# One row product by halves, first units by tiles, norm spread one unit later: three reorderings in a 256-token two-block network on Trainium2

## The reference

```python
def _rmsnorm(x, g):
    y = xf * lax.rsqrt(jnp.mean(xf * xf, axis=-1, keepdims=True) + RMS_EPS)
    return (y * g)

def _swiglu(h, w_in, w_out):
    gate, up = jnp.split(h @ w_in, 2, axis=-1)
    return (jax.nn.silu(gate) * up) @ w_out

for i in range(DEPTH):            # nsa mixer, then wkv mixer
    ...
    x = x + jnp.concatenate([mix, cross], axis=-1) @ w_o[i]
    x = x + _swiglu(_rmsnorm(x, norm2[i]), w_ffn_in[i], w_ffn_out[i])
x = _rmsnorm(x, final_norm)
...                               # second_block: mixer, then
h = rmsnorm(x, ffn_pre_g[l])
x = x + rmsnorm(swiglu(h, w_gate[l], w_up[l], w_down[l]), ffn_post_g[l])
```

## Time and profile before

| what | value |
|---|---|
| median of 3 runs | 1194.93 us (1193.71 to 1199.79) |
| the profiled execution | 1196.21 us, span 1194.4 us |
| granted TensorE clock, mean | 0.988 of full |
| PE busy | 1158.1 us (97%) |
| DVE busy | 758.2 us (63%) |
| ACT busy | 603.2 us (51%) |
| chain that ended last | PE 87%, DVE 6%, ACT 3%, DMA 2%, issue 1% |

### The profile page before, as it was taken

One profiled execution on the slowest core, in us unless ns is written; L12 is line 12 of the kernel. 1 busy time (PEld: TensorE's weight loads), 2 busy tenths in 40 slices (PEclk: granted clock), 3 DMA queues, 4 the chain that ended last, 5 costly groups with the idle time before them and its releaser, 6 DMA issues.

```text
span 1194.4 us, 23500 instructions
## 1 busy us (share of the span) xinstructions
PE 1158.1 (97%) x9992; PEld 1079.9 (90%) x9992; DVE 758.2 (63%) x1292; ACT 603.2 (51%) x1029; POOL 32.0 (3%) x46
## 2 busy tenths in 40 slices
PE   6999999999999999999999999999999999999997
PEld 6999888999988988898789998889999998999986
DVE  5575656676736668766667675475754676767644
ACT  4665555444434673434354544364358755444533
POOL 0000000000000010340000000000000000000000
PEclk9999999999999998999899999999999999999999
DMA  9843124876554533001488765546654444777651
GB/s 280 247 128 103 71 72 137 225 198 190 199 188 146 178 106 106 3 3 39 112 217 219 202 188 204 182 119 203 183 183 127 140 144 127 191 201 188 202 186 71
DMA packets 218916, 185.38 MB, mean 155 GB/s; under 512 B 11266, under 2 KB 204048, under 8 KB 218684
## 3 DMA queue, kind: packets, MB, share of 16 engines
q1 hardware_dynamic: 217226, 181.50, 50.6%
q0 software_dynamic: 384, 1.05, 0.4%
q10 hardware_dynamic: 1202, 1.34, 0.3%
HBM read 181.77 MB, written 1.05 MB: 153 GB/s over the span
## 4 chain that ended last, share of the span: by engine, by line
PE 87%; DVE 6%; ACT 3%; DMA 2%; issue 1%; SPq 0%; DVEq 0%; ACTq 0%
PE bank L849 24%; PE bank L851 23%; PE bank L850 23%; DVE w_lo L2258 2%; PE bank L1422 1%; PE bank L836 1%; PE bank L1192 1%; PE bank L1203 1%; DMA rows_tm<-in_mem 1%; PE bank L1398 1%; DMA ring<-in_w_ffn_in 1%; PE bank L1406 1%; ACT w_hi L1745 1%; PE bank L1080 1%; PE bank L1054 1%
## 5 line engine op out<-in xcount | busy, mean ns | idle before, releaser
L2258 DVE TENSOR_TENSOR w_lo<-ring,w_hi 128x1024 fp32r<-128x1024 f32 (+2 forms) x332 | 380.3, 1187 | 235.8 <-ACT w_hi L1745 235.0
L1745 ACT ACTIVATE w_hi<-ring 128x1024 fp32r<-128x1024 f32 (+2 forms) x330 | 322.2, 1027 | 387.6 <-PE bank L851 371.9
L849 PE MATMUL bank<-act_pair,w_hi 128*128 128x256 f32 (+1 forms) x1503 | 421.2, 280 | 5.3 <-issue 3.4
L850 PE MATMUL bank<-act_pair,w_hi 128*128 128x256 f32 (+1 forms) x1503 | 417.4, 278 | 0.0
L851 PE MATMUL bank<-act_pair,w_lo 128*128 128x256 f32 (+1 forms) x1503 | 417.4, 278 | 0.0
L849 PEld LDWEIGHTS bank<-act_pair,w_hi 128*128 128x128 f32 (+1 forms) x1503 | 282.2, 188 | 9.4 <-issue 7.0
L851 PEld LDWEIGHTS bank<-act_pair,w_lo 128*128 128x128 f32 (+1 forms) x1503 | 282.3, 188 | 0.2
L850 PEld LDWEIGHTS bank<-act_pair,w_hi 128*128 128x128 f32 (+1 forms) x1503 | 282.3, 188 | 0.2
L849 PE MATMUL bank<-w_hi,act_pair 128*128 128x256 f32 (+1 forms) x448 | 140.6, 314 | 4.0 <-DVE w_lo L2258 1.6
L850 PE MATMUL bank<-w_lo,act_pair 128*128 128x256 f32 (+1 forms) x448 | 136.5, 305 | 0.0
L851 PE MATMUL bank<-w_hi,act_pair 128*128 128x256 f32 (+1 forms) x448 | 136.5, 305 | 0.0
(11 more groups left out here) (327 smaller groups left out, 1273.7 us busy)
## 6 DMA issues: line engine op xcount, KB each, us to landing
ring<-in_w_ffn_in SPq DMA_DIRECT2D x88, 512.0 KB, 5.2
ring<-in_w_in SPq DMA_DIRECT2D x28, 1024.0 KB, 5.2
ring<-in_w_ffn_out SPq DMA_DIRECT2D x22, 1024.0 KB, 4.8
ring<-in_rw_w_in SPq DMA_DIRECT2D x11, 1024.0 KB, 5.3
ring<-in_w_gate SPq DMA_DIRECT2D x22, 512.0 KB, 4.0
ring<-in_w_up SPq DMA_DIRECT2D x22, 512.0 KB, 5.2
ring<-in_w_down SPq DMA_DIRECT2D x11, 1024.0 KB, 4.8
ring<-in_w_o SPq DMA_DIRECT2D x8, 1024.0 KB, 4.8
```

What stands on the lines that cost most here:

```text
L849: pe.matmul(o, ahl[0], bhl[0], start=first, stop=False)
L850: pe.matmul(o, ahl[0], bhl[1], start=False, stop=False)
L1745: ins = act.activation(tiles[0], raw, copy)
L2258: ins = dve.tensor_tensor(tiles[1], raw, tiles[0], ALU.subtract)
```

## The change

Three things are done. First, the last row unit of `wo0`, `f0`, `wo1` and `f1` writes token tile 1 by feature halves, and reports the first half (semaphore half_done), so that DVE may add bank 2 before bank 3 is done; the two products that did this already count on with the same semaphore. Second, the first unit behind each boundary (`f0_in0`, `z9`, `f1_in0`, `sv0`, `f2_in0`) takes the feature tiles in the outer loop and its two column (or token) tiles in the inner one. Third, the spread of the row scales stands behind the second unit instead of the first in `f0`, `f1`, `f2` and z; in block 2 it stood there before.

```diff
@@ ffn_units
-            if j == 0:
+            if j == 1:
                 unit(f"scale_{tag}", upper=True)
@@ z units
-        if j == 9:
+        if j == 10:
             unit("scale_z", upper=True)
@@ block.tensor
+        def entry_unit(name, held, moving):
+
+            begin(name)
+            for k in range(KT):
+                tile_ready(k)
+                if k % (KT // PIECES) == 0:
+                    piece(name, k // (KT // PIECES))
+                for c in range(2):
+                    ins = product(bank_of(name)[:, c * S:(c + 1) * S], [a[:, k, c * P:(c + 1) * P] for a in held],
+                                  [a[:, k, :] for a in moving], k == 0 and c == 0, k == KT - 1 and c == 1)
+            ins.then_inc(unit_done, 1)
+
+        def fm_entry(name, act):
+            entry_unit(name, split(name, KT), act)
+
+        def tm_entry(name, act):
+            entry_unit(name, act, split(name, KT))
@@ row_unit
-            def tile_product(a, qt):
+            def tile_product(a, qt, halves=(0, 1)):
                 k = 2 * j + a
-                for half in range(2):
+                for half in halves:
@@
                 piece(name, 1)
-                for qt in range(QT):
+                for a in range(2):
+                    ins = tile_product(a, 0)
+                ins.then_inc(sem("tile0_done"), 1)
+                for half in range(2):
                     for a in range(2):
-                        ins = tile_product(a, qt)
-                    if qt == 0:
-                        ins.then_inc(sem("tile0_done"), 1)
+                        ins = tile_product(a, 1, (half,))
+                    if half == 0:
+                        ins.then_inc(sem("half_done"), 1)
             ins.then_inc(unit_done, 1)
@@ ffn, on PE
-            for j in range(FT):
+            fm_entry(f"{tag}_in0", fm_of[tag])
+            for j in range(1, FT):
                 (lead_unit if j in (1, 2, 5) else fm_unit)(f"{tag}_in{j}", fm_of[tag])
-                if j == 0:
+                if j == 1:
                     spread_scale(tag)
@@
-        fm_unit("z9", fm_of["z"])
+        fm_entry("z9", fm_of["z"])
+        fm_unit("z10", fm_of["z"])
         spread_scale("z")
-        fm_unit("z10", fm_of["z"])
         fm_unit("qm1", fm_of["z"])
@@
-        for j in range(4):
+        tm_entry("sv0", fm_of["b2"])
+        for j in range(1, 4):
             tm_unit(f"sv{j}", fm_of["b2"])
@@ post_squares, on ACT
-                        act.wait_ge(sem("half_done"), n + 1)
+                        act.wait_ge(sem("half_done"), ROW_PRODUCTS.index(final) + 1)
@@ product_tile, on DVE
             if i == 2:
+                dve.wait_ge(sem("half_done"), ROW_PRODUCTS.index(final) + 1)
+            if i == 3:
                 dve.wait_ge(*filled(final))
```

## The result

| | before | changed |
|---|---|---|
| median | 1196.15 us (1193.71 to 1199.79, 6 runs) | 1206.71 us (1203.67 to 1209.02, 6 runs) |
| profiled execution | 1196.21 us, span 1194.4 us | 1207.33 us, span 1205.5 us |
| granted TensorE clock, mean | 0.988 | 0.988 |

The ratio is 1.0089, 95% interval 1.0072 to 1.0107: 10.6 us slower, between 8.6 and 12.8. The direction was forecast; the size was 6.7, and 1206.7 us lies just above the range, which ended at 1206.5. Of the 5.1 us between 1201.6 and 1206.7, 1.2 are the median of before, which moved from 1194.93 to 1196.15 with more runs.

The account below looks back on a forecast made before the run. PE, busy 97% of the span, was taken as the bound. Losses of 1.78 us (f0), 0.7 (f1), 2.41 (z) and 1.81 (f2) summed to +6.7, giving 1201.6 us on the median; range 1198.8 to 1206.5.

Parts of the forecast that it names:

- The stops: At in2 of f0, f1, f2 and at qm1: PE waits for low halves queued behind DVE's copy, some 2.7 us each.
- The link taken from one row of block 2: At sv2: from the start of a pair of w_lo pieces to the matmul waiting for the first, 1.38 us.
- the late load of f1: At f1_in4: ACT already waited for its load until 621.97, so of f1's +1.71 us only +0.7 is left.
- The clock: At the four new stops: the granted clock stays at full speed, so a stop costs only its length.
- the boundary with its 16 transposes: Between last product and f0_in0: 3.34 us of thin work with a stop of 1.14, clock at 1.00; evidence for full clock.
- Rival 1: Clock falls behind the four stops, some 1.5 us each; one to four falls give 1203.1 to 1207.6; chance 0.20.
- The pace: Dense stretches at full clock: 90 or 87 matmuls in 10 us, 3% apart, taken to be set anew where PE stopped.
- Rival 2: Moved stops flip the pace of stretches, or small edit wins appear: sum about +4, 1198.9 us; chance 0.20.
- Edits one and two: At the boundaries: row unit by halves and tiles in order, each taken to win 0 us.
- edit one: At the boundaries: ACT's chain starts no sooner, so of 0.18 x 4 = 0.7 us at most, nothing is won.
- the diagonal: At the spread: PE's waits for it go when the spread moves, 0.40 to 0.60 us at three places.
- Rival 3: Low halves of in2 made ahead of DVE's copy: no stop, only wins of 3.1 us, 1191.8 us; chance 0.07.

Follow-up runs that it names:

- the spread alone: Only the spread of the row scales one unit later, halves and tile order as before, against before: 1209.68 us, ratio 1.0115.
- z alone: All three edits, low halves of unit three made ahead of the spread's copy in the feed-forward parts but not in z, against before: 1196.91 us, ratio 1.0000.
- the later loads: All three edits, low halves first everywhere, SP's five extra loads of f1 moved from in4 to in8, against before: 1196.86 us, ratio 0.9999.
- the kernel with work in the stops: All three edits plus 11 identity matmuls behind each of the four spreads, against before: 1204.13 us, ratio 1.0057; with 18 matmuls, 1206.84 us.
- the kernel with the low halves first: All three edits, but DVE makes the low halves of unit three ahead of the spread's copy, against before: 1194.72 us, ratio 0.9983.

## Why the prediction was wrong

**The stops: right.** Four places, cause, and length came as forecast: 7.4 us in the table against 7.7, spread to in2 in 3.07 against 3.20, and the waits for low halves 12.3 us in all against some 13. The link taken from one row of block 2, 1.38 us from the start of a pair of w_lo pieces to the matmul, measured 1.36 here (209.01 to 210.37). That the late load of f1 would swallow part of its stop was right too: ACT waits for that load until 629.08, 21.75 us behind in0, before 21.83, and the changed kernel has no wait at in4.

```profile
629.08 2.01 ACT L1768 ACTIVATE w_hi<-ring 128x1024 fp32r<-128x1024 f32 x2 [4.78 <-DMA ring<-in_w_ffn_in]
```

**The clock: the step that failed.** "So I price the new stops at full clock" is the wrong sentence. It put the clock into the sum at nothing. It rested on the boundary with its 16 transposes, a stop of 1.14 us inside 3.34 us of thin work, and gave the fall a chance of 0.20. A bare stop is another thing. Of ten stops of 2.46 to 2.6 us in the profiles of four kernels (the change, the spread alone, z alone, the later loads) the clock fell behind six; of the eight places with work in the stop it fell at none; and the 3.2 us between transposes and first unit went without a fall in all of them. With 1.6 us a fall and a chance of six in ten, four stops should have been priced 3.8 us higher; by the clocks of all executions, some 2 us higher. Then 6.7 becomes 10.5 or 8.7, and 10.6 was measured, between 8.6 and 12.8. Both prices are taken from these kernels after the fact, so the agreement is a consistency and no test. The 6.8 us of the kernel with work in the stops (4.5 to 9.2) are the forecast as it stood. Rival 1 had the mechanism and nearly the price (1.5 us a fall). The Trainium skill's rule in "TensorE: Matmul & The Clock Gate", Part 1, that only activity holds the full clock, spoke for that rival, and the six falls agree with it.

**The pace: partly there.** Rival 2 took the sum down in the main; in the profile the pace added. A window of the changed kernel in f2 behind the stop, the first matmul of f2_in5, and a window behind that:

```profile
1030.00:1040.00 10.00, 10.00 (x87) 10.00 (x86) 7.87 (x11) 3.42 (x7) 0.00 (x0) 1.00 0.73 216
```

```profile
1046.05 0.29 PE L857 MATMUL bank<-act_pair,w_hi 128*128 128x288 f32 x1
```

```profile
1050.00:1060.00 10.00, 10.00 (x90) 10.00 (x90) 6.81 (x10) 5.24 (x8) 0.00 (x0) 1.00 0.75 206
```

These are the two paces of the earlier trace rows. Before the `lead_unit` in5 the matmuls follow each other at 0.1178 us, from its first ones on at 0.1133, and PE did not stop between. The slow pace over in2, in3 and in4, 144 matmuls, costs 0.65 us: that is the 0.66 behind f2's stop, where the clock did not fall. In z, qm1 and z3 ran slowly behind the fall; that is some 0.4 of the 1.79 us. So the rival's premise, that a stop sets the pace anew, is only part of it: a lead unit ends the slow pace too, which kept the loss in f2 small.

**Edits one and two: right in the sum.** Nothing was taken for either, and neither can be measured. The reason given for edit one was wrong all the same: ACT was to start no sooner than 1.42 us behind the transposes, and it started at 1.29. The halves shorten the chain by 0.13 us, inside the bounds of 0 and 0.18. The tile order wins 0.3 us in a first unit, and the diagonal takes it back in f0, f1 and f2.

**Rival 3** was out by the trace, and the kernel with the low halves first shows it as it would have been: 2.0 us faster, where it had 3.1.

**The range** ended at three falls of a price that was 0.1 too low, counted from a median of before that was 1.2 us too low (the prediction's own 1.5 us for each of three falls gives 1206.1, not the 1206.5 that it names). 1206.7 is only 0.2 above its end; with a fall behind each of the four stops as likely as measured, it had to reach past 1208.

## What to carry to other kernels

When a result is moved later on one engine, look at what is queued behind its reader on the other: here DVE idled 5.41 us ahead of the copy with the next unit's halves waiting behind it, and two lines that put them first turned a loss of 10.6 us into a gain of 2.0 (0.2 to 3.9). A bare stop of 2.5 us in a dense stream of matmuls costs more than its length, here by an estimate 1.6 x 0.6 = 1 us more on average (0.5 and 1.2 for each stop by the clocks of the two kernels with four of them). Price it so, and where it can't be avoided, throwaway matmuls in it can win part of this back (3.8 us here, give or take 3.1), if they are shorter than the stop by their measured length. Compare the granted clock over many executions, not over one pair of profiles: a single pair had as much low clock before as after. A shorter first unit brings nothing as long as the unit behind it waits for something that does not come sooner.

## What was not expected of the hardware

- The clock fell behind six of ten bare stops of 2.46 to 2.6 us, and the same stop in the same place could go either way: behind f1's it fell in the change and held with the spread alone. In f0 it stayed at 0.50 for 3.4 us of dense work, 211.65 to 215.05.
- At full clock a matmul of 256 columns follows the last at 0.1133 us or at 0.1178. The same unit shows both: f0_in0 ran at 0.1178 in the change and at 0.1133 with 18 matmuls added later in the program. A stop can bring the slow pace (in2 of f2), but the pace also changes without one: in the twelve profiles PE came to a `lead_unit`, which begins with a matmul of 288 columns, 26 times at the slow pace without a stop or a spread between, and ran at the fast one behind it 26 times; of 46 reached at the fast pace none turned slow. What brings the slow pace is open.
- An identity matmul of 128 x 128 in full f32 is two records of 0.11 us in the trace, where the instruction is one.
